# Layer norms by token tile, the router's work in a new order, and stand-in products for TensorE, in a two-layer decoder trunk

## The reference, cut to what matters

```python
for i in range(DEPTH):                       # DEPTH = 2
    j = i // 2
    if i % 2 == 0:
        mix = attn_deltanet_mixer(x, ...)    # window attention and gated DeltaNet
    else:
        mix = mamba2_mixer(x, ...)           # state-space mixer
    x = layer_norm(DEEPNORM_ALPHA * x + mix, ln_g[i, 0], ln_b[i, 0])
    if i % 2 == 0:
        ffn = swiglu(x, ffn_w_gate[j], ffn_w_up[j], ffn_w_down[j])     # width 2816
    else:
        ffn = moe_swiglu(x, moe_w_router[j], ...)                      # 8 experts of width 3584
    x = layer_norm(DEEPNORM_ALPHA * x + ffn, ln_g[i, 1], ln_b[i, 1])

def swiglu(x, w_gate, w_up, w_down):
    return (jax.nn.silu(x @ w_gate) * (x @ w_up)) @ w_down

def moe_swiglu(x, w_router, b_router, w_gate, w_up, w_down):
    logits = (xt @ w_router) + b_router
    top_val, top_idx = lax.top_k(logits, TOP_K)                        # TOP_K = 2
    gates = jax.nn.softmax(top_val, axis=-1)
    combine = jnp.sum(one_hot(top_idx, N_EXPERTS) * gates[..., None], axis=1)
    for e in range(N_EXPERTS):
        out = out + combine[:, e:e + 1] * swiglu(xt, w_gate[e], w_up[e], w_down[e])
```

## Time and profile before

| what | value |
|---|---|
| median of three runs | 1714.66 us |
| the profiled execution | 1714.81 us |
| its span | 1712.9 us |
| mean granted clock of TensorE | 0.960 |
| TensorE busy | 1620.3 us, 95% |
| VectorE busy | 1291.9 us, 75% |
| ScalarE busy | 968.2 us, 57% |
| GpSimd busy | 38.2 us, 2% |
| moved by transfers | 441.01 MB, 257 GB/s on average |

### The profile page before, as it was taken

One profiled execution on the slowest core, in us unless ns is written; L12 is line 12 of the kernel. 1 busy time (PEld: TensorE's weight loads), 2 busy tenths in 40 slices (PEclk: granted clock), 3 DMA queues, 4 the chain that ended last, 5 costly groups with the idle time before them and its releaser, 6 DMA issues.

```text
span 1712.9 us, 22538 instructions
## 1 busy us (share of the span) xinstructions
PE 1620.3 (95%) x8800; PEld 1382.2 (81%) x8800; DVE 1291.9 (75%) x1084; ACT 968.2 (57%) x826; POOL 38.2 (2%) x35
## 2 busy tenths in 40 slices
PE   6989899996998899899999999999999999999995
PEld 5878499996998677788888888888888888888883
DVE  3766645455676557688888898998988988988995
ACT  3323234442443542477776776776767776777772
POOL 3000000002000000000000000000000000000000
PEclk8999999998999868799999999999999999999997
DMA  9050256554443005699999999999999999999990
GB/s 323 29 197 1 88 184 195 178 189 147 148 150 122 26 25 194 227 367 375 349 368 356 353 358 342 365 360 343 362 369 336 363 354 349 368 364 345 363 342 26
DMA packets 210749, 441.01 MB, mean 257 GB/s; under 512 B 7172, under 2 KB 57568, under 8 KB 210656
## 3 DMA queue, kind: packets, MB, share of 16 engines
q1 hardware_dynamic: 208656, 434.42, 71.0%
q10 hardware_dynamic: 1440, 4.78, 0.8%
q0 software_dynamic: 560, 0.48, 0.2%
HBM read 438.61 MB, written 1.05 MB: 257 GB/s over the span
## 4 chain that ended last, share of the span: by engine, by line
PE 85%; DVE 9%; ACT 3%; issue 1%; POOL 1%; DMA 1%; POOLq 0%; ACTq 0%; DVEq 0%
PE ps L2071 18%; PE ps L2073 18%; PE ps L2072 18%; PE ps L1629 4%; PE ps L1630 4%; PE ps L1631 4%; DVE w_lo L1017 2%; DVE arena L1046 2%; PE ps L1622 2%; PE ps L2066 1%; PE ps L2096 1%; ACT w_hi L656 1%; PE ps L1886 1%; PE ps L1885 1%; PE ps L1887 1%
## 5 line engine op out<-in xcount | busy, mean ns | idle before, releaser
L1437 DVE TENSOR_TENSOR w_lo<-raw,w_hi 128x2048 fp32r<-128x2048 f32 x252 | 577.3, 2291 | 90.3 <-ACT w_hi L873 85.6
L873 ACT CAST w_hi<-raw 128x2048 fp32r<-128x2048 f32 x252 | 482.6, 1915 | 174.8 <-PE ps L2073 160.5
L2071 PE MATMUL ps<-w_hi,xg_hi 128*128 128x512 f32 x672 | 269.1, 401 | 4.8 <-DVE xg_lo L1494 3.5
L1017 DVE TENSOR_TENSOR w_lo<-raw,w_hi 128x2048 fp32r<-128x2048 f32 (+1 forms) x73 | 164.6, 2260 | 135.1 <-ACT w_hi L656 135.0
L2073 PE MATMUL ps<-w_hi,xg_lo 128*128 128x512 f32 x672 | 263.4, 392 | 0.0
L2072 PE MATMUL ps<-w_lo,xg_hi 128*128 128x512 f32 x672 | 262.5, 391 | 0.0
L656 ACT CAST w_hi<-raw 128x2048 fp32r<-128x2048 f32 (+1 forms) x73 | 136.6, 1877 | 165.4 <-PE ps L1631 107.0
L1629 PE MATMUL ps<-xT_hi,w_hi 128*128 128x256 f32 x768 | 219.7, 286 | 5.5 <-DVE xT_lo L1010 5.2
L1630 PE MATMUL ps<-xT_lo,w_hi 128*128 128x256 f32 x768 | 219.3, 286 | 0.0
L1631 PE MATMUL ps<-xT_hi,w_lo 128*128 128x256 f32 x768 | 219.3, 286 | 0.0
L1437 DVE TENSOR_TENSOR xT_lo<-raw,xT_hi 128x2048 fp32r<-128x2048 f32 x84 | 192.3, 2290 | 31.6 <-ACT xT_hi L873 31.2
(11 more groups left out here) (366 smaller groups left out, 2268.6 us busy)
## 6 DMA issues: line engine op xcount, KB each, us to landing
raw<-in_moe_w_gate SPq DMA_DIRECT2D x112, 1024.0 KB, 5.9
raw<-in_moe_w_up SPq DMA_DIRECT2D x112, 1024.0 KB, 6.6
raw<-in_moe_w_down SPq DMA_DIRECT2D x112, 1024.0 KB, 6.2
raw<-in_ssm_w_in SPq DMA_DIRECT2D x20, 1024.0 KB, 5.4
raw<-in_ffn_w_gate SPq DMA_DIRECT2D x11, 1024.0 KB, 5.3
raw<-in_ffn_w_up SPq DMA_DIRECT2D x11, 1024.0 KB, 5.3
raw<-in_ffn_w_down SPq DMA_DIRECT2D x11, 1024.0 KB, 4.8
raw<-in_even_w_in SPq DMA_DIRECT2D x10, 1024.0 KB, 13.3
```

What stands on the lines that cost most here:

```text
L873: act.copy(e_hi((n + 2 * odd) % CUT_E), raw[:, i, :]).then_inc(sem("hi_made"), 1)
L1017: TTO(w_lo[:, c, 0:size], raw[:, i, 0:size], w_hi[:, c, 0:size].bitcast(F32), ALU.subtract).then_inc(d_lo_made, 1)
L1437: TTO(e_lo(c), raw[:, n % RAW, :], e_hi(c).bitcast(F32), ALU.subtract).then_inc(lo_made, 1)
L2071: mm(out_ap, hi, whi, start=start, stop=False)
```

## The change

Five things are put together.

1. Seam A: the token halves of tile 0 are cast and lowered between the weight pieces (`turn_high` and `turn_low` are told which quarters to do).
2. Seam B: the last hidden block gets its own buffer, `last_hi` and `last_lo` (the other half of `ehT_hi` and `ehT_lo`), so its silu waits for one piece less. The last two down-projections are written by quarters (`ffn_rows`): three quarters of step 9, tile 0 of step 10, the last quarter of step 9, tile 1 of step 10. Only one weight piece, not two, is lowered before norm 1, and the other two behind the tokens; ScalarE casts the tokens ahead of its third weight piece and of the loads for the next norm.
3. Seam C: VectorE copies the turned tokens before it lowers piece 0, lowers piece 1 behind the selection rows, then takes the gathered tokens, pieces 2 and 3, and only then the rest of the router's work. ScalarE's order follows. The opening counts `e_h`, `ehT_made` and `oe_lo_made` are given in front of the gathered tokens; `e_added` stays behind `yacc`.
4. `keep_running(bank, n)`: n products of 512 columns (bf16, identity by identity) into a bank whose content nobody reads afterwards. They stand at ten lines in the seams, which run twelve times in all, 104 products together.
5. The last pair of feed-forward steps is written out behind the loop, which now runs four times, not five.

```diff
@@ scalar
             act.wait_ge(sem("out_proj"), 2)
-            for n in range(N0, N0 + CUT):
-                dense_high(n, n % RAW_D, n % CUT, n // RAW_D + 1)
+            n = N0
+            dense_high(n, n % RAW_D, n % CUT, n // RAW_D + 1)
+            turn_high(1, (0, 1))
+            n = N0 + 1
+            dense_high(n, n % RAW_D, n % CUT, n // RAW_D + 1)
+            turn_high(1, (2, 3))
             load_ln(1)
-            turn_high(1)
+            n = N0 + 2
+            dense_high(n, n % RAW_D, n % CUT, n // RAW_D + 1)
...
-                act.wait_ge(d_piece_used, 3 * step + (CUT + N0 + 2))
+                act.wait_ge(d_piece_used, 3 * step + (CUT + N0 + (1 if isinstance(step, int) else 2)))
...
-            for n in range(N1, N1 + CUT):
+            for n in range(N1, N1 + 2):
                 dense_high(n, n % RAW_D, n % CUT, n // RAW_D + 1)
+            turn_high(2)
             load_ln(2)
-            turn_high(2)
+            n = N1 + 2
+            dense_high(n, n % RAW_D, n % CUT, n // RAW_D + 1)
...
                 act.wait_ge(d_piece_used, CUT + NPRE)
+                turn_copies(3, (0, 1))
                 cut_high(0, (0, 0), 0)
-            turn_copies(3, (0, 1))
-            if limit >= 5:
-                cut_high(1, (0, 0), 0)
-                cut_high(2, (0, 0), 0)
...
             act.activation(g1[:, :, :], dm[:, :, :], ACT.Exp).then_inc(sem("rt_e"), 1)
+            cut_high(1, (0, 0), 0)
...
+            gathered_high((0, 0))
+            cut_high(2, (0, 0), 0)
             cut_high(3, (0, 0), 0)
-            gathered_high((0, 0))
@@ vector
-            for n in range(N0, N0 + 2):
-                dense_low(n, n % RAW_D, n % CUT)
-            turn_low(1)
+            turn_low(1, (0, 1))
+            dense_low(N0, 0, 0)
+            turn_low(1, (2, 3))
+            dense_low(N0 + 1, 1, 1)
             dense_low(N0 + 2, 2, 2)
...
-            ffn_h(0, FSTEPS - 1)
+            ffn_h(0, FSTEPS - 1, last_hi, last_lo, 1)
             if limit >= 3:
-                for n in range(N1, N1 + 2):
-                    dense_low(n, n % RAW_D, n % CUT)
+                n = N1
+                dense_low(n, n % RAW_D, n % CUT)
             layer_norm(1, [(sem("ffn_tile"), 1), (d_piece_used, CUT + N1)])
...
             turn_low(2)
-            n = N1 + 2
-            dense_low(n, n % RAW_D, n % CUT)
+            for n in range(N1 + 1, N1 + CUT):
+                dense_low(n, n % RAW_D, n % CUT)
@@ tensor
+            def keep_running(bank, n):
+
+                for _ in range(n):
+                    mm(ps[:, bank, :], identb[:, :], over_heads(identb[:, :], 4), start=True, stop=True)
...
-            turn(1)
+            turn_tile(1, 0)
+            keep_running(2, 20)
+            turn_tile(1, 1)
...
+            keep_running(4, 11)
             open_banks()
...
+            with pe.Fori(0, FSTEPS // 2 - 1) as i:
+                ffn_pair(i)
+                ffn_down(6 * i + (N0 + 7), 1, 2 * i + 1)
+            ffn_pair(FSTEPS // 2 - 1)
+            n, c, step = N1 - 2, (N1 - 2) % CUT, FSTEPS - 2
+            ffn_rows(n, c, step, 0, (0, 1), hT_hi, hT_lo, False)
+            ffn_rows(n, c, step, 1, (0,), hT_hi, hT_lo, False)
+            ffn_rows(n + 1, (n + 1) % CUT, step + 1, 0, (0, 1), last_hi, last_lo, True).then_inc(sem("ffn_tile"), 1)
+            ffn_rows(n, c, step, 1, (1,), hT_hi, hT_lo, False).then_inc(d_piece_used, 1)
+            ffn_rows(n + 1, (n + 1) % CUT, step + 1, 1, (0, 1), last_hi, last_lo, True).then_inc(d_piece_used, 1)
+            keep_running(0, 8)
+            turn_tile(2, 0)
+            keep_running(2, 19)
+            turn_tile(2, 1)
+            keep_running(4, 7)
...
+            pe.wait_ge(sem("y_summed"), 3)
+            keep_running(7, 4)
             for t in range(TT):
                 turn_tile(3, t)
+                keep_running(7, 4)
...
                 token_major(ps[:, 4, t * E:(t + 1) * E], w_rt, t).then_inc(sem("logits"), 1)
+                keep_running(7, (7, 10)[t])
...
+            keep_running(7, 5)
...
             gather((0, 0))
+            keep_running(7, 5)
```

## The result

The changed kernel took 1688.76 us (median of 4 runs, 1685.93 to 1695.59), the kernel before 1715.41: a ratio of 0.9855, 95% interval 0.9831 to 0.9879. The forecast was 1693.1, with a range of 1688 to 1701. The profiled runs are 1685.93 and 1714.81 us, so 28.9 us apart where the sum said 21.7. The seams give that sum or somewhat less, and a part of the kernel that nobody edited gives the rest.

A forecast was written before the change was run, and what follows sets the result against it. TensorE was taken to be full in feed-forward, state-space projections and experts, leaving only the seams between: 3.8 + 8.3 + 9.6 = 21.7 us off 1714.81 gives 1693.1. Own range 1690 to 1697; 8 in 10, 1688 to 1701.

The forecast's parts named there:

- the sum: The gains at the three seams added up: 21.7 us off the profiled 1714.81 us, giving 1693.1.
- A: Before the feed-forward part: TensorE starts 2.1 us earlier and the kept clock saves 1.7, together 3.8 us.
- B: Behind the feed-forward part: state-space products start 6.8 us earlier and the kept clock saves 1.5, together 8.3 us.
- C: Norm, router and gather before the experts: 8.0 us earlier start, 2.7 by clock, less 1.1 of stall, together 9.6 us.
- Stall at piece 4: Start of the experts: TensorE waits 1.1 us for VectorE's weight piece 4, bounds nothing and 3.9 us.
- the tail: Rest of the router's work on VectorE, 3.9 us, said to lie in the gather's shadow before and now ahead of piece 4.
- (1): Seam C: the clock falls there, costing 1.6 us for a short fall, 8.1 for a whole one; 1698, chance 0.17.
- (2): Experts: they are bound by their transfers, so seam C gives nothing; 1702.7 us, chance 0.05.
- (3): Seam B: the feed-forward part doesn't end early, as silu or its buffer still waits; 1697.5 us, chance 0.05.
- (4): All seams: the stand-ins themselves delay, each taking 0.43 us with the clock down; 1727.4 us, chance 0.03.

The follow-up runs named there:

- experiment 7: The changed kernel run once more, unaltered, which gave its second profile: 1694.73 us (1685.29 to 1698.12), ratio 0.987.
- experiment 3: Changed kernel with seam A's old order of casts and low parts put back, stand-in products kept: 1698.65 us, ratio 0.9907.
- experiment 4: Changed kernel with seam B's old silu wait, single hidden-block buffer, down-projection order and two weight pieces before the norm put back, stand-ins kept: 1701.23 us, ratio 0.9912.
- experiment 1: Changed kernel with all 104 stand-in products left out, its orders kept: 1716.08 us, ratio 1.001 to the kernel before.
- experiment 5: Changed kernel with seam C's old order of router work and weight pieces put back, stand-ins kept: 1695.96 us, ratio 0.9904.
- experiment 9: Changed kernel with seam A's stand-ins doubled (20 to 40, 11 to 22): 1698.34 us, ratio 0.989.
- experiment 6: Changed kernel with 48 more stand-ins in the state-space mixer: 1685.57 us (1682.12 to 1688.56), ratio 0.9825.
- experiment 10: Changed kernel with 48 more stand-ins in the state-space mixer and GpSimd's join behind VectorE's third low piece of seam B: 1688.43 us, ratio 0.984.

## Why the prediction was right, and where it was not

The fair comparison for the sum is the second profile of the changed kernel: in it as in the profile before, the offset products ran at half clock. Spans 1712.9 and 1693.6: 19.3 us, against 21.7. The medians of the two groups (experiment 7) say 20.2 and 21.8. So the sum was about right at an equal length of the offset products. That the measured median fell 4.3 us below the forecast is in good part the draw: three of its four runs were of the lower group.

- **A, 3.8.** Earlier start 2.20 (forecast 2.1). Clock: no 0.50 behind the seam, and experiment 3 prices it at 1.5 when it comes back (1.7). Right in size. But the stand-ins did not earn it: in both profiles without their work N1-F is 194.89 all the same, and with them and the longer gap of the old order the clock falls. It was the shorter gap.
- **B, 8.3.** N1-F fell by 6.88, of which 5.2 to 5.4 are left after A's clock, and S-N1 by 1.36: 6.5 to 6.7 (6.8), experiment 4 says 7.1. The 1.5 of clock was there at the seam and was given back in this profile: O-S is 173.51 against 173.45, with the clock at 0.50 again inside the projections. In the first profile it was kept: no such fall, and O-S 171.87. Why it falls there in one run and not in another is as open as for the offset products, for TensorE is busy all through the 10 us ahead of it.

```profile
430.80:437.50 6.70, 6.70 (x33) 6.70 (x33) 3.83 (x8) 3.19 (x4) 0.00 (x0) 0.50 0.50 157
```

- **C, 9.6.** E-N2 21.89 to 13.97: 7.92 (8.0); end-E 1.2 shorter in this profile and 1.6 in the first (2.7 - 1.1 = 1.6). From the experts' first product to the start of the second gather the timelines have 107.4 us (781.75 - 674.34) and before 109.2 (810.66 - 701.49): 1.8 less, 1.6 forecast. Stall at piece 4: 0.5 to 0.7 (1.1). Total right; its make-up was not. I had the tail "in the gather's shadow", and thought most of C to be the clock. Orders alone give 2.0 of the 7.9 us (experiment 1), the clock alone 2.6 (experiment 5), both 7.9: each hides behind what the other leaves.
- **Sum.** 2.20 + 6.88 + 1.36 + 7.92 + 1.2 = 19.6, less 0.3 from a later end of norm 0.
- **The failed step** was outside the sum: "other stretches with half clock shift with their start and add 2 us either way". One stretch alone, the offset products, is worth 8.8 us by its clock (21.37 to 12.59), of which 2.3 come back behind them (N2-Y 66.39 against 64.08): 0.7 up to the sums of squares, where TensorE now waits 1.82 us for VectorE's weight piece, 0.95 in the sums (11.09 against 10.14, clock 0.64 against 0.70), and 0.7 in the output products behind these, of which more run at 0.50. The 6.5 us left are the distance of the two groups (1688.7 and 1695.5). The first profile had it at full clock. This 6.5, 1.6 less between S and O, an end of norm 0 that comes 1.0 earlier and 0.4 less in the experts make the 28.8 us between the spans out of 19.3: luck of that run, not work of the seams. The row that would have warned me is above: 22.00 us at 0.51 in the profile before.
- **Rivals.** (1) no: clock 1.00 through seam C in both profiles; the run that lay 7 us above the others fits the upper group of experiment 7. By the prediction's reading, the rule of the Trainium skill (TensorE: Matmul & The Clock Gate, Part 4) that transposes don't count as busy in the same way would have put C at half clock; measured is 1.00, with eight transposes (1.09 us) at a time between groups of stand-ins. That refutes the reading and not the rule, for the stand-ins ran on both sides. The rows that the prediction held against the rule are weaker than it says: behind the same 16 transposes, at 110.15 in the first profile of the changed kernel, the clock was 0.50 from 115.2 to 118.6, and it fell there in five of the twelve profiles; in the other seven, the one before and the second of the changed kernel among them, it stayed up. So the rule stays open here. (2) no: TensorE starts 27 us earlier and still shows the same experts (E to end). (3) no: N1-F. (4) no, but its price is real (experiment 9).

## What to carry to other kernels

Before a change to one seam is priced, look for stretches elsewhere that run at half clock though TensorE is never idle in them. Here one was worth as much as a seam (8.8 us by itself, 6.5 in the whole) and came and went from run to run, and one profile of each kernel credited it to the edit. Time each kernel often enough to see its groups, and compare group with group. Two fixes at one seam can each be worth little alone and the full sum together, since each is hidden by what the other removes. An experiment that takes instructions out also moves the code behind it; keep their number and take away their work.

## What the runs showed of the hardware

- At a jump of the experts' long loop TensorE is idle for 0.6 to 1.1 us in most profiles here, and for 1.97 to 2.77 us at one of the two jumps in experiments 3, 5, 6 and 10. Those longer ones don't hang on TensorE's program: in experiments 3 and 5 it is the changed kernel's own (0.69 and 0.78 us in its first profile), and experiments 6 and 10 share one, with the long jump first in the one and second in the other. In experiment 1 the idle time is 6.13 and 5.65 us, and from E to the end it takes 15.6 us more than the changed kernel.
- VectorE and GpSimd held each other up where both read two operands from on-chip memory (the low weight piece and the join of the token parts). The piece that started first took its 2.28 us; the join behind it 6.60 = 2.1 of waiting + 4.5; the two pieces behind the join 8.91 = 4.5 of waiting + 4.4. The Trainium skill (SBUF — State Buffer, section "SBUF: two separate sides") calls the port pair that the two share an exclusive lock, held for the whole instruction. The trace agrees to 0.2 us.
- One-column products did not hold the clock: 11.1 us at 0.64 in the changed kernel for 32 of them (64 rows). With three 512-column products behind each group of four it stayed up (1.00 in experiment 6, and no fall there in experiment 10).
